# Compression pages of a decoder step: read as whole rows and turned by VectorE in 32x32 blocks, with a turn of the sample attention reordered

## The reference, cut to what matters

```python
def compressed_attend(q, kv_all, pos, pe, w1, w2):
    ...
    blocks = kv_all[:, idx] + jnp.transpose(pe, (1, 0, 2))[:, :, None, :]
    flat = jnp.transpose(blocks, (0, 1, 3, 4, 2, 5)).reshape(b, n_cmp, 2, NSA_KV_GROUPS, CMP_BLOCK * HEAD_DIM)
    hid = jax.nn.gelu(jnp.einsum('bncgf,cfh->bncgh', flat, w1))
    comp = jnp.einsum('bncgh,chd->bncgd', hid, w2)
    ...
```

## Time and profile before

| what | value |
|---|---|
| median of 3 runs | 1561.75 us (1561.35 to 1565.24) |
| the profiled execution | 1560.01 us, its span 1558.0 us |
| granted clock, mean | 0.979 |
| busy: PE / DVE / ACT / POOL | 92% / 31% / 19% / 7% of the span |
| the four turns | start at 269.86, 334.66, 402.32 and 470.61 us; the merge products begin at 532.62 us |
| the experts | from about 616 us to the end |
| packets under 512 B | 30962 of 99146 |
| chain that ended last | PE 69%, DMA 19%, DVE 5%, ACT 3%, SyncE's queue 1% |

### The profile page before, as it was taken

One profiled execution on the slowest core, in us unless ns is written; L12 is line 12 of the kernel. 1 busy time (PEld: TensorE's weight loads), 2 busy tenths in 40 slices (PEclk: granted clock), 3 DMA queues, 4 the chain that ended last, 5 costly groups with the idle time before them and its releaser, 6 DMA issues.

```text
span 1558.0 us, 21396 instructions
## 1 busy us (share of the span) xinstructions
PE 1437.8 (92%) x7528; PEld 650.1 (42%) x7528; DVE 475.2 (31%) x1084; ACT 292.1 (19%) x609; POOL 101.8 (7%) x217
## 2 busy tenths in 40 slices
PE   5998989888888899999999999999999999999986
PEld 3445554656656446433333333333333333333332
DVE  1113363344243464413213213213213213213214
ACT  2002432343333403010111011011011010110112
POOL 1002001422310000000000000000000000000000
PEclk9998999999989999999999999999999999999999
DMA  7217734676757774999999999999999999999993
GB/s 252 108 54 191 266 98 156 199 238 170 222 160 233 244 281 192 414 429 427 429 429 427 429 429 427 429 429 427 429 429 427 429 429 427 429 429 427 428 429 128
DMA packets 99146, 507.56 MB, mean 326 GB/s; under 512 B 30962, under 2 KB 45650, under 8 KB 73970
## 3 DMA queue, kind: packets, MB, share of 16 engines
q1 hardware_dynamic: 91026, 483.28, 77.7%
q0 software_dynamic: 8064, 23.60, 4.8%
HBM read 500.35 MB, written 10.62 MB: 328 GB/s over the span
## 4 chain that ended last, share of the span: by engine, by line
PE 69%; DMA 19%; DVE 5%; ACT 3%; issue 3%; SPq 1%; ACTq 0%; DVEq 0%
PE PS L1336 21%; DMA arena<-in_w_gate_up 18%; PE PS L1363 9%; PE PS L1310 5%; PE PS L343 5%; PE PS L599 3%; PE PS L529 3%; PE PS L2000 3%; PE PS L1302 3%; PE PS L1198 2%; PE PS L1054 2%; PE PS L352 1%; PE PS L572 1%; PE PS L1944 1%; ACT arena L762 1%
## 5 line engine op out<-in xcount | busy, mean ns | idle before, releaser
L1336 PE MATMUL PS<-arena 128*64 128x512 f32 x2048 | 457.7, 596 | 24.3 <-DMA arena<-in_w_gate_up 23.5
L1336 PEld LDWEIGHTS PS<-arena 128*64 128x64 f32 x2048 | 141.3, 137 | 308.9 <-issue 259.5
L1363 PE MATMUL PS<-arena 128*64 128x512 f32 x1024 | 226.0, 594 | 3.2 <-DVE arena L1819 2.3
L1778 DVE TENSOR_SCALAR arena<-PS 128x512 f32<-128x512 f32 x32 | 22.1, 691 | 489.5 <-PE PS L1345 488.6
L1363 PEld LDWEIGHTS PS<-arena 128*64 128x64 f32 x1024 | 72.2, 137 | 150.2 <-issue 147.5
L529 PE MATMUL PS<-arena 128*128 128x128 f32 (+1 forms) x624 | 99.2, 300 | 37.8 <-ACT arena L762 14.1
L529 PEld LDWEIGHTS PS<-arena 128*128 128x128 f32 (+1 forms) x624 | 73.5, 151 | 61.2 <-ACT arena L762 20.9
L1302 PE MATMUL PS<-arena 128*128 128x512 f32 (+1 forms) x192 | 79.4, 618 | 6.0 <-ACT arena L1506 6.0
L1310 PE MATMUL PS<-arena 128*128 128x512 f32 (+1 forms) x180 | 84.2, 609 | 0.0
L343 PE MATMUL PS<-arena 128*128 128x512 f32 (+1 forms) x192 | 78.6, 571 | 0.6 <-ACT arena L2185 0.6
L1491 ACT ACTIVATE arena<-arena 128x512 f32<-128x512 f32 x32 | 20.2, 630 | 293.1 <-DVE arena L1778 293.1
(11 more groups left out here) (286 smaller groups left out, 1315.2 us busy)
## 6 DMA issues: line engine op xcount, KB each, us to landing
arena<-in_w_gate_up SPq DMA_DIRECT2D x128, 2048.0 KB, 22.2
arena<-in_w_down SPq DMA_DIRECT2D x64, 2048.0 KB, 21.8
arena<-in_w_in SPq DMA_DIRECT2D x9, 2048.0 KB, 11.6
arena<-in_cache_diff_k SPq DMA_DIRECT2D x64, 256.0 KB, 4.4
arena<-in_cache_diff_v POOLq DMA_DIRECT2D x64, 256.0 KB, 4.1
arena<-in_cache_sel_kv SPq DMA_DIRECT2D x64, 128.0 KB, 2.3
arena<-in_cache_cmp_kv POOLq DMA_DIRECT2D x64, 64.0 KB, 4.1
arena<-in_cache_cmp_kv SPq DMA_DIRECT2D x64, 64.0 KB, 2.6
```

Of the source, the lines that this page charges most:

```text
L1336: last = nc.tensor.matmul(bank(2 + role + 2 * u)[64 * h:64 * h + 64], hTm[:, k, BS * u:BS * u + BS], gu_w[:, k, D * role + 512 * h:D * rol ...
L1363: last = nc.tensor.matmul(bank(6 + u)[64 * h:64 * h + 64], aT[u][:, c % 4, 64 * (c // 4):64 * (c // 4) + 64], down_w[u][c // 4][:, c % 4, ...
```

## The change

Compression pages are read as whole rows of 1 KB, 128 KB a page: for b = 0 by SyncE's queue, for b = 1 by GpSimd's, eight transfers each a turn. Row 4k + r of a page goes to partition 32r + k. VectorE transposes each 32x32 block from `cmp_raw`, now with room for one sequence, into `cmpT`, which has a place of its own. The first layer's weights are loaded once more, in the order of rows that fits (`w1_quads`, 16 transfers on SyncE's queue). A turn has 34 groups. The pages of a turn are turned by VectorE in the turn before: for b = 0 in two halves (keys after the first layer's key products, values after the second layer's results), for b = 1 after `dif_mask(1)`. The order of TensorE, ScalarE and VectorE in a turn is new.

```diff
-        cmpT = at(18432, 4, 2, CS // 2, PAST // CS)
+        cmpT = at(14336, 16, 4, PAST // CS)
-        cmp_raw = at(14336, NPAGE, 512)
+        cmp_raw = alloc(NPAGE, 256)
-        L_TP = 42
+        L_TP = 34
-        joined = bank(2)[:, 0:128]
+        joined = bank(3)[:, 0:128]
...
+        def cmp_pages(eng, i, b, first=False):
             cmp_d = io["cache_cmp_kv"][0].rearrange("n p c g d -> n p (c g d)")
+            for pg in range(NPAGE):
+                page = page_of(eng, i, b, pg)
+                if b or not first:
+                    eng.wait_ge(cmp_turned, i * 16 + (8 * b - 7 + pg) if not first else pg + 1)
+                eng.dma_start(cmp_raw[:, pg],
+                              cmp_d[bass.ds(page, 1)].rearrange("a (k r) n -> (a r) k n", r=4)).then_inc(cmp_in[2 * b + pg // 4], 16)
...
             with sp.Fori(1, PAIRS_OF_SEQ) as i:
-                cmp_pages(i)
+                cmp_pages(sp, i, 0)
                 dk_pages(i, 0)
...
             with pool.Fori(1, PAIRS_OF_SEQ) as i:
-                odd_rows(i)
+                cmp_pages(pool, i, 1)
                 values_in(i, 0)
...
# GpSimd, prompt: before the copy of merge gate 11
+                if n == 11:
+                    cmp_pages(pool, 0, 1, True)
...
# TensorE, a turn
                 dif_scores(0)
-                (eight groups of compression pages, 593)
+                pe.wait_ge(cmp_turned, i * 16 + 16)
+                hidden(0, range(8))
+                sel_t(0)
+                hidden(0, range(8, 16))
+                sel_t(1)
+                hidden(1, range(16))
                 dif_probs_t(0)
-                (32 first-layer products, dif_values(0), sel_t(0), join(0), sel_t(1))
                 pe.wait_ge(l_gelu, i + 1)
                 (second layer, 611 and 614)
-                (two window groups)
+                dif_values(0)
                 pe.wait_ge(l_kv_out, i + 1)
                 (compressed scores, 622)
+                (two window groups)
+                join(0)
                 (selection scores, 629 and 631)
+                pe.wait_ge(l_pn, i + 1)
+                nc.tensor.matmul(bank(2)[:, 0:NCC], const("rsum"), pn, start=True, stop=True).then_inc(l_grp, 1)
                 (window scores, 634 and 636)
-                (l_pn and rsum, 638 and 639)
...
# ScalarE, a turn: opening
-                ev(0, 2)
                 exp(3, 1, e_sel, s_sel, lsum[:, 3:4])
-                ev(4, 6, 8, 10)
-                (both GELUs after l_hid, table(ACT.Exp), ev(12, 14), square(0), ev(16), exp(1, ...), ev(17, 18, 19, 20))
+                ev(0)
+                table(ACT.Gelu_apprx_tanh, 0)
+                gelu(0)
+                ev(2)
+                gelu(1)
+                table(ACT.Exp, 1)
+                ev(4, 6, 8)
+                exp(1, 2, pn, s_cmp, lsum[:, 1:2])
+                square(0)
+                ev(9, 10, 11, 12, 13)
                 exp(2, 3, e_sel, s_sel, lsum[:, 2:3])
...
# VectorE
+            def turn_pages(i, b, cs=(0, 1)):
+                for pg in range(NPAGE):
+                    if pg % 4 == 0:
+                        dve.wait_ge(cmp_in[2 * b + pg // 4], i * 64 + 64)
+                    m0, m1 = 4 * cs[0], 4 * cs[-1] + 4
+                    out = cmpT[:, 8 * b + m0:8 * b + m1, :, 8 * pg:8 * pg + 8].rearrange("p m r n -> p m n r")
+                    st(V.transpose(out, cmp_raw[:, pg, 32 * m0:32 * m1].rearrange("p (m d) -> p m d", d=32)), cmp_turned if 1 in cs else None)
...
                 dif_mask(0)
-                ev(1, 3, 5, 7)
+                ev(1, 3)
+                if not final:
+                    dve.wait_ge(l_hid, i * 2 + 1)
+                    turn_pages(i + 1, 0, (0,))
                 past(dve, l_exp, i * 5 + 1)
+                ev(5)
                 (second-layer results, 868 and 869)
+                if not final:
+                    turn_pages(i + 1, 0, (1,))
                 dif_scale(0)
                 negmax(1, s_cmp)
+                ev(7)
                 (compressed softmax)
+                dif_joined(0)
+                (block choice, 881 to 896)
                 past(dve, l_sc, i * 3 + 2)
-                (block choice, 881 to 896)
...
                 dif_mask(1)
+                if not final:
+                    turn_pages(i + 1, 1)
...
# SyncE, prompt: after load_chunk(9), ahead of the 64 loads of gS
+            sp.wait_ge(ph_full, 2)
+            (16 loads "w1_quads" of 32 partitions x 8 x 512 B)
+            cmp_pages(sp, 0, 0, True)
# VectorE, prompt: in step 7, between weigh and maxima
+                if s == n - 1:
+                    first_pages(dve, st)
# VectorE, after the copies of the first keys
+            turn_pages(0, 1)
```

More of the change, by code:

```diff
@@ L586, in turn, with hidden @@
                 pe.wait_ge(l_cur, (i + 1) * 3)
-                dif_scores(0)
[L588 to L592, removed]
-                        tp(i, G_CMP + 4 * b + k, [(cmp_raw[:, 4 * b + k, 128 * m:128 * m + 128], 128 * m) for m in range(4)], const("phase"))
-                dif_probs_t(0)
-                l_out_done(pe, i, G_CMP + 7)
-                for c in range(2):
-                    for l in range(CB // 2):
-                        last = nc.tensor.matmul(bank(2)[:, 4 * NCC * c:4 * NCC * (c + 1)], w1[:, c, l, :],
-                                                cmpT[:, 2 * c:2 * c + 2, :, l % (CS // 2), 2 * l // CS:2 * l // CS + NCC],
-                                                start=(l == 0), stop=(l == CB // 2 - 1))
-                last.then_inc(l_hid, 1)
-                dif_values(0)
-                sel_t(0)
+                def hidden(c, steps):
+                    for l in steps:
+                        last = nc.tensor.matmul(bank(2 + c)[:, 0:4 * NCC], w1[:, c, l, :], cmp_window(c, l), start=(l == 0), stop=(l == CB // 2 - 1))
+                    if CB // 2 - 1 in steps:
+                        last.then_inc(l_hid, 1)
+                dif_scores(0)
+                pe.wait_ge(cmp_turned, i * 16 + 16)
[4 more added lines that the diff above has]
+                hidden(1, range(16))
+                dif_probs_t(0)
                 pe.wait_ge(l_gelu, i + 1)
-                join(0)
-                sel_t(1)
-                pe.wait_ge(l_osq, i * 2 + 1)
                 for g in range(2):
@@ L623, in turn @@
                 last.then_inc(l_cmp, 1)
-                l_out_done(pe, i, G_WIN + 1)
+                for b in range(2):
+                    pe.wait_ge(win_in[b], (i + 1) * 16)
+                    tp(i, G_WIN + b, [(win_raw[:, b, h, 0:128], 128 * h) for h in range(4)])
+                join(0)
+                l_out_done(pe, i, G_SEL + 3)
                 past(pe, l_exp, i * 5 + 1)
@@ L1914, in _ @@
             load_chunk(9)
+            sp.wait_ge(ph_full, 2)
+            for c in range(2):
+                for r, e in ((r, e) for r in range(4) for e in range(2)):
+                    load(sp, "w1_quads", w1[32 * r:32 * r + 32, c].rearrange("p (s e) h -> p s e h", e=2)[:, :, e],
+                         io["w_cmp1"][0, c].rearrange("(s r e p) h -> r e p s h", r=4, e=2, p=32)[r, e])
+            cmp_pages(sp, 0, 0, True)
             sp.wait_ge(gate_rows, 16)
```

137 lines of the change are left out of this document (54 added, 83 removed).

## The result

| | before | after |
|---|---|---|
| median (4 runs each, beside each other) | 1561.64 (1561.35 to 1565.24) | 1577.30 (1576.55 to 1578.79) |
| ratio, 95% interval | | 1.0094 [1.0077, 1.0112] |
| profiled execution, its span | 1560.01, 1558.0 | 1577.84, 1575.9 |
| granted clock, mean | 0.979 | 0.961 |
| turns start at | 269.86, 334.66, 402.32, 470.61 | 273.45, 348.61, 420.34, 491.65 |

I forecast 1550 and a gain. The loss arises in the loop over turns: turns of 75.2, 71.7 and 71.3 us, where 63.7, 65.7 and 65.7 were forecast. (The merge products of the kernel before begin at 524.45; the 532.62 that stands ahead of the prediction is the start of their third stretch.)

A forecast was written before the change was run, and what follows sets the result against it. From the second turn on SyncE's queue, not TensorE, was taken to set the pace. A fourth turn starting 5.6 us earlier and 5.9 shorter gave -11.5: 1548.5 profiled, median 1550; range 1542 to 1561.

The forecast's parts named there:

- fourth, against before: Last turn of the loop: with no pages to turn and no table load at its old opening, 5.9 us shorter.
- 16 issues of 1.45 become eight of about 1.09, as selection pages have the same 128 rows of 1 KB.: SyncE's queue, compression pages for b = 0: cheaper issues make the queue 14.5 us shorter a turn.
- the hole: SyncE's gap at the loop's jump back, 7.4 us before: taken as 4 us, between 2.3 and 7.4.
- some 20: Prompt, SyncE's queue: 16 weight loads and eight more pages, some 20 us, cost nothing, between 0 and +3.
- rival (c): VectorE's early wait for b = 0 pages decides, with late pages and loops of 72.2 us: 1567, slower; chance 0.08.
- `G_O`'s wait: TensorE before group `G_O`, turns one to three: a pause of about 4 us (44.0 to 48.4), none in the fourth.
- the pause for the table load: Opening of a turn: TensorE idles about 2 us while ScalarE does the second GELU and loads the exponential table, 1.28.
- scores for b = 1: Middle of a turn: these scores start 38.6 us into it, 45.5 before.
- no wait for keys: Turns two and three: keys for b = 0 come in time, so TensorE's wait (3.85 us in the third) goes.
- rival (d): VectorE's transposes run at half rate, 0.75 us a page instead of 0.40: -5, 1556; chance 0.07.
- the forecast's own case: Whole kernel: -11.5 us, a median of 1550, its own range 1545 to 1555; chance 0.50.
- The clock terms: Lower clock after TensorE's waits: 2.0 us added a turn for the pause before `G_O`, 1.0 after the later `dif_values(0)` wait.

The follow-up runs named there:

- plain rows: The changed kernel with each compression page, on SyncE's and GpSimd's queues, read in the order of its rows, leaving out the token sorting: 1551.2, ratio 0.9930.
- run with only b = 1 moved: The changed kernel with VectorE's b = 1 transposes moved from behind `dif_mask(1)` to behind the sum of the branches, transfers untouched: 1569.8, ratio 1.0054.

## Why the prediction was wrong, point by point

| step | forecast | measured | us lost |
|---|---|---|---|
| first turn starts | 269.9 | 273.45 | 3.6 |
| first turn | 63.7 | 75.2 | 11.5 |
| second | 65.7 | 71.7 | 6.0 |
| third | 65.7 | 71.3 | 5.6 |
| fourth, against before | -5.9 | -1.9 | 4.0 |
| merge and experts | 0 | -1.3 | -1.3 |

Forecast -11.5, measured +17.8 (1577.84 against 1560.01): the rows make up the 29.3 between them to the rounding.

*The step that failed: "16 issues of 1.45 become eight of about 1.09, as selection pages have the same 128 rows of 1 KB."* The destination is alike, the source is not. From the start of the selection issues, the first page was issued 30.1 us later (329.67 to 359.77), where 32.0 was forecast; the eighth came 13.4 behind it and not 7.6, and took 3.82 and not 2.4 to land. That is 5.3 us later in all, and the second and third turns are 6.0 and 5.6 too long. Seven steps at 1.92 instead of 1.09 are 5.8 of that and the landing is 1.4; the earlier first page, without the hole, gave 1.9 back. I looked for a row with the same bytes and rows, not for one with the same shape of pattern. The rule on the number of engines speaks against this very edit, and the prediction did not weigh it.

*The first turn* was to have no late pages. The same slow pages stood in the prompt's queue (13.88 us) together with 16 weight loads (13.12), 27 us where "some 20" was forecast as hidden. SyncE asked for the second turn's first page at 282.37; before, that issue began at 274.30:

```profile
274.30 23.60 SPq L415 DMA_DIRECT2D arena<-in_cache_cmp_kv  x16
```

In that turn the eighth page was there only at 304.7. With plain rows the first was asked for at 276.33, and TensorE did not wait in that turn. The cost of the prompt's queue appeared one stage later. I had asked only when its data was first used, not what stands behind it on the queue.

*The first turn's late start is another matter.* SyncE's store of the gates (line 1889 before, 1900 after) is issued at 170.19 before and at 173.78 after, so the 3.6 us are lost before the new loads are issued. The granted clock over 100 to 180 was 0.91 before and 0.83 after. The run with only b = 1 moved has the same code up to there and issued that store at 170.56, with 0.91. The table's 3.6 is thus chiefly the clock of that one execution. All kernels with this prompt start their first turn between 270.4 and 273.7, which is 0.5 to 3.9 later than the kernel before; how much of this is the change's own is not shown.

*Where the mechanism was seen and held to be unlikely:* rival (c), with a chance of 0.08, is what happened, at loops near its 71.5. Its time was 1567, as it kept the first turn short and gave the fourth its full gain. It named issues of 1.45 "because rows are scattered by four", and a hole of 8. The pages were slower than that and the hole was absent.

*Right:* `G_O`'s wait (4.4 forecast, 5.06); the pause for the table load (about 2, 1.69); scores for b = 1 at 39.0 into the fourth turn (38.6); no wait for keys. VectorE's transpose, which no row had shown, takes 0.47 a page (eight in 3.76 in the first turn) and 0.25 a half, against 0.40 and 0.27: rival (d) is out. With plain rows the forecast's own case came about, 1551.2 against 1550, with waits of 2.21 and 1.44 before `dif_values(0)` where 2.4 was reckoned. That the totals are so near is luck in part: its three turns were 3.8 us shorter than forecast and what follows the turns 1.2, while its first turn started 3.5 late and its fourth was 4.0 too long.

*Mis-sized:* the hole, forecast 4 within 2.3 to 7.4, was 1.4. The change itself had cut the loop's body from 337 instructions to 288; the prediction compared the hole with how full the DMA queues are and did not count the body. The page that it cites gives no length for the stall, so that the trace agreed with it in place only. The fourth turn gained 1.9 and not 5.9. TensorE's timeline of the kernel before, fourth turn, has the scores for b = 1 and the last `dif_values`:

```profile
513.93 1.93 PE L553 MATMUL PS<-arena 128*32 128x512 f32 x16
...
522.21 1.95 PE L572 MATMUL PS<-arena 128*32 128x128 f32 x64 [0.72 <-DVE arena L751]
```

The scores start 43.3 into that turn, and 39.0 in the changed kernel. Behind them 10.5 us remained to the first merge product before, and 12.9 after. The difference from the forecast is the clock: the granted clock over the whole turn was 1.00 before and 0.91 after, and the last `dif_values` took 1.95 and 3.64. The run with only b = 1 moved has the same fourth turn in code. It ran it at 1.00, with scores 37.4 in and 10.5 behind them, 47.97 us in all: 5.9 less than before, as forecast. The clock terms were low throughout: the mean fell from 0.979 to 0.961, and each wait of 9 to 11 us is followed by `dif_values` at 3.64 too.

## What to carry to other kernels

When a transfer's price is taken from a neighbour, match the whole access pattern, its slowest dimension first, and not only bytes and rows; a DMA share far under 1 while an engine waits for that data is the sign that its transfers are on few engines, or that its issues are slow, and here it was both. A wait that is added to an in-order engine is priced by what stands behind it in its list: here waits of 9 to 11 us a turn vanished when the waiting work was put where its data is there anyway. And check each term of a queue for what it pushes behind it, one stage later than its own data is needed.

## What the runs showed of the hardware that was not expected

- A 128 KB page from HBM with a source of slowest dimension 4, on SyncE's queue: four packets in flight, at most a share of 0.27 and 95 GB/s, 3.8 to 7.9 us to landing; with plain rows 2.1. One packet of 1 KB takes about 50 ns either way. SyncE's issue of it takes 0.62 and not 0.33, and a page-number read right behind it 0.64 and not 0.27. Why these two are stretched was not settled.
- GpSimd's queue takes the same pattern with less harm: eight pages 1.3 apart in either form, a median of 3.7 to landing against 2.5 with plain rows.
- A loop of SyncE's whose body has 337 to 388 instructions stands 4.6 to 6.9 us at each jump back; with 233 to 313 it stands 0.3.
- VectorE turns 128x256 float32 in blocks of 32x32 in 0.47 us, with strided writes.
